# Recurrence of an RWKV-7 layer: the inverse's second direction moved to the array's off-diagonal quarters, work banks in two rotating pairs, side products for all 768 tokens at once

## What the reference computes

```python
def rwkv7_scan(S0, r, decay, k, v, kk, a, reverse):
    def step(S, inp):
        r_t, w_t, k_t, v_t, kk_t, a_t = inp
        sa = jnp.einsum('bhvk,bhk->bhv', S, -kk_t)
        S = (S * w_t[:, :, None, :] + sa[..., None] * (kk_t * a_t)[:, :, None, :]
             + v_t[..., None] * k_t[:, :, None, :])
        return S, jnp.einsum('bhvk,bhk->bhv', S, r_t)
...
    for d, rev in enumerate((False, True)):
        S_c, yc_d = rwkv7_scan(S0, r_c, d_c[d], k_c[d], v_c, kk_c, a_c[d], rev)
        _, yl_d = rwkv7_scan(S_c, r_l, d_l[d], k_l[d], v_l, kk_l, a_l[d], rev)
```

## Time and profile before

| | us |
|---|---|
| median of three executions | 2581.54 (2580.11 to 2587.41) |
| the profiled execution, its own time | 2585.16 |
| its span in the trace | 2583.6 |
| recurrence in the trace, its first products to its last | about 455 to 1121 |
| TensorE busy over the span | 2260.9 (88%) |

### The profile page before, as it was taken

How to read it: one execution, slowest core, us unless ns; L and a number is a source line. 1 busy time by engine, 2 the same in 40 slices (tenths; PEclk the granted TensorE clock), 3 DMA queues, 4 the chain that set the end, 5 groups by cost and what they waited for, 6 DMA issues and landing times. The chain is left out here.

```text
span 2583.6 us, 60917 instructions
## 1 busy us (share of the span) xinstructions
PE 2260.9 (88%) x26659; PEld 1830.6 (71%) x26659; DVE 1146.9 (44%) x1601; ACT 799.4 (31%) x1329; POOL 451.9 (17%) x335
## 2 busy tenths in 40 slices
PE   5899994788888998869799999999696778899998
PEld 3677782677777777757688888888563436688887
DVE  4633322666776667532422222222386652433333
ACT  2223322344334433221522112211433331542231
POOL 0222312644555446300000000000120000000000
PEclk8799896899999999989899999999798989999999
DMA  9566652000000000031122212121110002233332
GB/s 307 173 209 185 192 179 70 23 24 10 30 30 24 30 10 10 10 140 47 49 65 65 72 51 65 57 75 37 44 50 0 0 0 82 73 100 95 98 103 85
DMA packets 261822, 191.73 MB, mean 74 GB/s; under 512 B 11610, under 2 KB 252132, under 8 KB 261092
## 3 DMA queue, kind: packets, MB, share of 16 engines
q1 hardware_dynamic: 261604, 188.45, 24.0%
HBM read 170.60 MB, written 17.83 MB: 73 GB/s over the span
## 5 line engine op out<-in xcount | busy, mean ns | idle before, releaser
L486 DVE TENSOR_TENSOR ffn_lo<-ffn_raw,ffn_hi 128x1024 fp32r<-128x1024 f32 (+1 forms) x120 | 159.8, 1332 | 571.4 <-ACT ffn_hi L481 571.4
L493 PE MATMUL bank<-operand_hi,ffn_hi 128*128 128x512 f32 (+1 forms) x1056 | 378.9, 359 | 24.6 <-DVE operand_lo L455 24.4
L494 PE MATMUL bank<-operand_lo,ffn_hi 128*128 128x512 f32 (+1 forms) x1056 | 378.1, 358 | 0.0
L495 PE MATMUL bank<-operand_hi,ffn_lo 128*128 128x512 f32 (+1 forms) x1056 | 375.0, 355 | 0.0
L481 ACT CAST ffn_hi<-ffn_raw 128x1024 fp32r<-128x1024 f32 (+1 forms) x120 | 136.4, 1137 | 531.3 <-PE bank L495 531.1
L1569 POOL TENSOR_TENSOR lvl<-sc_b,level_mask 128x512 f32<-128x512 f32 x144 | 192.9, 1354 | 320.4 <-PE bank L1158 297.5
L493 PEld LDWEIGHTS bank<-operand_hi,ffn_hi 128*128 128x128 f32 x1056 | 200.4, 190 | 61.8 <-issue 22.4
L495 PEld LDWEIGHTS bank<-operand_hi,ffn_lo 128*128 128x128 f32 x1056 | 200.2, 190 | 29.9
L494 PEld LDWEIGHTS bank<-operand_lo,ffn_hi 128*128 128x128 f32 x1056 | 200.7, 190 | 27.2
L494 PE MATMUL bank<-ffn_g_lo,ffn_hi 128*128 128x512 f32 (+1 forms) x528 | 188.0, 356 | 0.0
L493 PE MATMUL bank<-ffn_g_hi,ffn_hi 128*128 128x512 f32 (+1 forms) x528 | 187.4, 355 | 0.0
(11 more groups left out here) (244 smaller groups left out, 4519.3 us busy)
## 6 DMA issues: line engine op xcount, KB each, us to landing
mod_raw<-in_mod_w SPq DMA_DIRECT2D x96, 512.0 KB, 6.1
ffn_raw<-in_ff_w SPq DMA_DIRECT2D x88, 512.0 KB, 3.9
ffn_raw<-in_ff_w SPq DMA_DIRECT2D x32, 704.0 KB, 4.5
proj_raw<-in_rw_wr SPq DMA_DIRECT2D x8, 512.0 KB, 4.5
proj_raw<-in_rw_wk SPq DMA_DIRECT2D x8, 512.0 KB, 4.6
proj_raw<-in_rw_wv SPq DMA_DIRECT2D x8, 512.0 KB, 4.9
rwkv_out_raw<-in_rw_wo SPq DMA_DIRECT2D x8, 512.0 KB, 4.3
qk_w_raw<-in_at_wq SPq DMA_DIRECT2D x8, 512.0 KB, 3.8
```

The source lines that it names most:

```text
L486: signal(eng, eng.tensor_tensor(self.lo[s][:, 0:k_tiles, :], self.raw[s][:, 0:k_tiles, :], self.hi[s][:, 0:k_tiles, :].bitcast(F32), ALU.s ...
L493: pe.matmul(out, w[0], x[0], start=first, stop=False)
L494: pe.matmul(out, w[0], x[1], start=False, stop=False)
L495: return pe.matmul(out, w[1], x[0], start=False, stop=last)
```

## The change

In `t` and `y` the first direction stays on the diagonal quarters and the second goes to the off-diagonal ones. The product `t` of direction 1 lands on the other head's partitions, so `y` needs the inverse of direction 1 with its halves exchanged: ScalarE makes that copy after every level but the last (`swap`, two copies of 64 partitions by 256 columns, 5 times per group), and `y` waits for it. The inverse is stored direction by direction. Scores, turned keys, values, `t`, `y` and all side products rotate through two pairs of banks (`WORK = c.pair`, 1024 columns each), so there is one rotation instead of two. A side product is made for 768 tokens at once, in one place of the table, and read by one instruction. The products with values leave `y`: those for the next step's right-hand side are issued in `rhs`, those for its output in `u`, those for its state in `sy`, each between matmuls of the diagonal quarters. The turned keys are copied by one instruction of 1024 columns instead of two of 512.

```diff
+        inv_s = [sb(f"inverse_swapped{s}", [P, GROUP, CH]) for s in range(2)]
...
-        Y_BANK, CHAIN, B_BANK, K_BANK, WORK = c.bank[0:2], c.bank[2:4], c.bank[4], c.bank[5], c.bank[6:8]
+        Y_BANK, CHAIN, WORK = c.bank[0:2], c.bank[2:4], c.pair
...
-        PLACES = ({0: (0,), 1: (1, 2), 2: (3,), 3: (36, 4), 4: (5,), 6: (37, 8), 7: (9,), 8: (10,), 9: (6, 11), 11: (7,)},
+        MAPS = {2: 0, 4: 1, 8: 2, 10: 3}
+        PLACES = ({0: (0,), 1: (1,), 2: (2,), 4: (36, 4), 6: (37, 8), 8: (10,), 9: (6,)},
                   {0: (12, 13), 2: (14,), 3: (15,), 4: (16,), 5: (17,), 6: (18, 22), 9: (19, 23)},
-                  {0: (24, 25), 3: (26, 27), 9: (33, 34)})
+                  {0: (24, 25), 3: (26, 27), 9: (33,)})
...
-                if k in (4, 5):
-                    side(t, "y_norm", k - 4)
-                if k in (7, 8):
-                    side(t, "gate", k - 7)
+                if k == 4:
+                    side(t, "y_norm")
+                if k == 7:
+                    side(t, "gate")
...
+                            elif kind == "score":
+                                pe.wait_ge(masked, 4 * rest[0] + 2 * rest[1] + 2)
+                            elif kind == "side":
+                                was_read(pe, self.use, *rest)
                             else:
-                                was_read(pe, self.use, *rest)
+                                pe.wait_ge(tok_copied, self.use.of("turn", kind, *rest) + 1)
                         return WORK[n % 2]
...
-                        for w in range(2 * GROUP):
-                            for h in range(2):
-                                mm = pe.matmul(bank[half(h), w * CH:w * CH + CH], lvl[G.parity][n % 2][half(h), w, :],
-                                               inv_t[G.parity][half(h), w, :], start=True, stop=True)
+                        for q in range(GROUP):
+                            for e in range(2):
+                                w, out = GROUP * e + q, slice(512 * e + q * CH, 512 * e + q * CH + CH)
+                                for h in range(2):
+                                    mm = pe.matmul(bank[half(h ^ e), out], lvl[G.parity][n % 2][half(h), w, :],
+                                                   inv_t[G.parity][half(h), w, :], start=True, stop=True)
                         mm.then_inc(t_ready, 1)
...
                         pe.wait_ge(t_copied, self.use.of("t", G.g, n) + 1)
-                        if step:
-                            self.early_waits(*step)
-                        for w in range(2 * GROUP):
+                        pe.wait_ge(x_swapped, self.use.of("x", G.g, n - 1) + 1)
+                        for q in range(GROUP):
                             for h in range(2):
-                                mm = pe.matmul(bank[half(h), w * CH:w * CH + CH], t_sb[G.parity][half(h), w, :],
-                                               inv[G.third][half(h), w, :], start=True, stop=True)
-                            if step and w < 6:
-                                self.early_part(*step, w)
+                                pe.matmul(bank[half(h), q * CH:q * CH + CH], t_sb[G.parity][half(h), q, :],
+                                          inv[G.third][half(h), q, :], start=True, stop=True)
+                            for h in range(2):
+                                mm = pe.matmul(bank[half(h), 512 + q * CH:512 + q * CH + CH],
+                                               t_sb[G.parity][half(1 - h), GROUP + q, :], inv_s[G.parity][half(1 - h), q, :],
+                                               start=True, stop=True)
                         mm.then_inc(x_ready, 1)
...
+                    def swap(self, G, n):
+
+                        for h in range(2):
+                            ins = a.copy(inv_s[G.parity][half(1 - h)], inv[G.third][half(h), GROUP:2 * GROUP, :])
+                        ins.then_inc(x_swapped, 1)
+
+                    def level0(self, G):
+                        act.wait_ge(level0_done, G.g + 1)
+                        self.swap(G, 0)
+
+                    def y(self, G, n):
+                        if n < LEVELS - 1:
+                            act.wait_ge(x_added, self.use.of("y", G.g, n) + 1)
+                            self.swap(G, n)
```

More of the change, by code:

```diff
@@ L873, in score @@
             def score(G, i):
-                use.take("bank", "score", G.g, i)
+                use.take("work", "score", G.g, i)
                 E.score(G, i)
             def turn_keys(G):
-                use.take("bank", "keys", G.g), use.take("turn", "keys", G.g)
-                use.take("copy", "b", G.g), use.take("copy", "k", G.g)
+                use.take("work", "keys", G.g), use.take("turn", "keys", G.g)
                 E.turn_keys(G)
@@ L883, in turn_values @@
                 if G.j < 2:
-                    use.take("bank", "values", G.g), use.take("turn", "values", G.g), use.take("copy", "v", G.g)
+                    use.take("work", "values", G.g), use.take("turn", "values", G.g)
                     E.turn_values(G)
```

372 lines of the change are left out of this document (188 added, 184 removed).

## The result

The changed kernel takes 2613.74 us (median of 4 runs, 2602.59 to 2623.28), the kernel before 2583.36 beside it (4 runs, 2580.11 to 2587.41): 1.0114 times the time, 95% interval 1.0081 to 1.0146. The prediction had 2554 and 2518 to 2586. The profiled execution took 2602.59 us and is the fastest of its four; its span is 2601.0.

The account below looks back on a forecast made before the run. TensorE was taken to bound only some slots, a loop over four engines the others. Terms 20 + 6 + 1 + 4 - 1 - 2 = 28 us off 2585.16 gave 2557, median 2554, range 2518 to 2586.

Parts of the forecast that it names:

- The product: In the inverse, each 32-row `t` or `y` takes 0.50 us instead of 0.94, saving 0.44 us.
- the floor of 25 ns a matmul: For `t` and `y`, a skill's minimum start-to-start gap: 32 rows at least 0.80 us, saving 0.14; the prediction rejected it.
- the ceiling: Most TensorE time the shorter products could save: 240 products, 106 us.
- The value products: Moved from `y` into `rhs`, `u` and `sy`, taken to cost 0; if not covered, 36 us in 96 steps.
- The exchange: ScalarE's two copies after a level: 0.63 us each pair, 76 us in all, hidden except in two places.
- One rotation: Side products wait more for banks; in the readout slot delays of 0.5, 1.6 and 1.5 us, partly paid back.
- the prediction's slower rival: Whole-width side products ahead of the state update lengthen readout slots about 3 us, side-work slots about 1: 2592, chance 0.15.
- The clock: Over the slots, less TensorE work lowers the granted clock; taken as 2 us lost.
- the prediction's bound: Over the slots, the granted clock falls from 0.98 to 0.89, with 39 us kept for it.
- The sum: All slots, prologue, last readout and clock together: 28 us gained.
- The slot without side work: That kind of slot gains 2.1 us of 21.23, coming to 19.1 us.

Follow-up runs that it names:

- first step's wait away, exchanges at `t`'s copy: Changed kernel without TensorE's first-step wait for the previous step's state, each exchange moved right ahead of the next level's `t` copy: 2585.9 us.
- diagonal, first step's wait away: Changed kernel with both inverse directions on diagonal quarters, no exchange, and no first-step wait for the previous step's state: 2599.6 us.
- mended, diagonal: The mended kernel with both directions on the diagonal quarters again and no exchange: 2594.8 us, ratio 1.0028.
- mended: Changed kernel without the first step's wait, exchanges at `t` copies, readout slots' first scores behind `u`, bonus work later: 2577.6 us, ratio 0.9969 against before.
- changed, fillers of 64 columns: Changed kernel with 8 unused 64x64 matmuls ahead of each of two waits per chunk step: 2666.4 us, ratio 1.0325.
- mended, fillers of two columns: The mended kernel with 16 unused two-column matmuls ahead of each of two waits per chunk step: 2728.8 us, ratio 1.0535.

## Why the prediction was wrong, point by point

**The product** was right: a `t` of 32 rows is over in 0.46 us (start of what follows; predicted 0.50):

```profile
820.34 0.68 PE L1156 MATMUL bank_pair<-inverse_t,lvl 64*64 64x64 f32 x32
820.80 0.43 PE L1255 MATMUL bank<-rhs,inverse 64*64 64x64 f32 x8
```

and the floor of 25 ns a matmul from the Trainium skill, "TensorE: Matmul & The Clock Gate", section "Back-to-back issue gap", doesn't hold for four quarters, as the prediction had argued from the earlier trace rows.

TensorE's busy time fell by 62 us and not by the 106 of the ceiling. Part of the difference is the clock: at half speed a record of a diagonal `t` starts 52 ns after the one before it, at full speed 28. By an estimate from that, 83 us more at half speed with TensorE three quarters busy add some 30 us of busy time.

**The value products** at 0: right for the products, shown by moving them on the kernel before. The wait that came with them in the first step is a term of its own, below.

**The exchange** is the step that failed. The prediction sized it a little low (0.82 us a pair where it had 0.63 and at most 0.8; 403 ns a copy) and looked at what stands behind it in two places, the last step and the slot from 802.62. It did not look at what is *queued behind it* in the others. In the readout slot that is the square, on which the variance, TensorE and the next `rhs` hang. Its words "the exchange runs beside the 0.71 us transpose and is hidden" consider only `y` and leave out ScalarE's queue. The prediction had the sum for the variance 1.0 us later, by the banks; it came 2.8 us later against the copy of `u`, and the slot took 29.4 us in place of 26.2. Moving that one exchange gave back 25 us on the kernel before, moving all gave 26 in the changed one, of a loss of 29.

```profile
L1490 ACT COPY inverse_swapped<-inverse 64x256 f32<-64x256 f32 x226 | 91.1, 403 | 137.4 <-DVE inverse L1370 134.3 <-DVE inverse L1358 1.3
```

Of that row the busy 91.1 us tells little, and neither does the sum of 137.4 us in which ScalarE sat idle ahead of it: on the kernel before it is 153.4 us with the exchanges in this order and 143.3 with one of them behind the square, and those 10 us went with 20 us of the stage. The price lies in the few waits with urgent work behind them. With the exchanges at the copies the same row of that kernel reads

```profile
L1499 ACT COPY inverse_swapped<-inverse 64x256 f32<-64x256 f32 x226 | 91.2, 404 | 4.1
```

**One rotation** was priced at little outside the readout slot. Diagonal quarters, no exchange, no first step's wait, against the kernel before with its value products moved: 1.0056 against 0.9996, some 15 us for the rotation and the whole-width pieces together. By slots, readout 28.1 in place of 26.7, side work 31.3 or more in place of 30.5, the third kind level. That is the mechanism of the prediction's slower rival in part (its 3 and 1 us), but the pieces put back made it worse, so what costs is most likely the banks that the scores and keys lost, and not the width. The two differ in more than that, the wide copy of the turned keys for one, which no run tried alone. One of the places, the scores ahead of `u`, is seen in the trace and was put right there: 0.18%, 5 us, by ratios within each other's intervals.

**The first step's wait** was in the diff and missing in the prediction: 5 to 11 us (0.21% with the quarters, 0.41% without, each between ratios whose intervals overlap).

**The clock** came out near the prediction's bound, not as its term: the slots fell to 0.92 (0.89 was the bound) and half-speed time rose from 21 to 104 us. What that costs in all was not isolated. In the slots of side work it can be read: four without half-speed time took 28.8 to 29.7 us, the two with 6.8 and 10.2 us of it 32.5 and 32.1, so some 7 us for both. It is not the main reason for the long readout slots, since two thirds of it stayed in them when they became short.

**The sum**, by the ratios along one path of single steps from before: value products moved -0.04%; rotation and whole width, diagonal, +0.60%; quarters with the exchanges at the copies (which holds the pauses and the clock) -0.63%; the exchanges put where the change has them +1.00%; the first step's wait +0.21%. That is 1.14%, 29 us slower. The prediction had -28 us for all of it. The quarters brought 16, and three other parts took 47. Each step carries an interval of about 0.2% or more, and another order of the steps could share the sum out differently: on the kernel before, the exchanges alone cost 1.66%.

**The slot without side work**, predicted at 19.1, took 24.52 at full clock. There the answer is not in any queue. Its waits:

```profile
PE bank_pair L1166 <- issue: 3.6, 5, 1.9
PE bank_pair L1156 <- issue: 2.5, 3, 1.6
PE bank L1199 <- issue: 1.5, 1, 1.5
PE bank_pair L1143 <- issue: 0.7, 1, 0.7
```

8.3 us in all. Some 2 of them, at `y`, are the usual wait for `t`'s copy, which shows as "issue" before too: 1.5 in the same slot. The others, 6.4 us in five places, are pauses at a matmul that waits for no semaphore, four of them inside a product, as in this one of 32 rows. They are more than the 5.4 us by which the slot missed its prediction, and are described below.

```profile
1051.38 0.33 PE L1156 MATMUL bank_pair<-inverse_t,lvl 64*64 64x64 f32 x8
1052.43 0.58 PE L1156 MATMUL bank_pair<-inverse_t,lvl 64*64 64x64 f32 x24 [0.73 <-issue]
```

## What to carry to other kernels

Before an instruction that waits is put on an engine with room, write down what that engine issues next and who waits for *that*, for every place in which it is issued; the average load says nothing of it. Put such an instruction where its input is already there, right ahead of the copy whose reader also needs it.
When several uses share one rotation of buffers, look for a pair of uses that now wait for the same event, and issue the one on the critical path first.
Where an engine idles at an instruction that waits for no semaphore, lay the idle time beside the packets that carry its instructions before looking for the cause in the data.
Test a change of several parts by putting each part alone on the old kernel: here two such runs cleared one part and convicted another whose price had been taken from its duration.

## What the hardware did that was not expected

**Columns don't matter in a small product on two quarters.** 32 matmul records of 64 rows and 2 columns take 1.10 us (above), as long as 32 of 64 columns on the diagonal. On four quarters 32 of 64 columns take 0.46 to the next start. So at full clock the time goes with the instructions and with how many quarters take turns. The same section of the Trainium skill's "TensorE: Matmul & The Clock Gate" gives one gap of about 25 ns for 1 to 64 columns; from the first start of a product to its last, the traces have 28 ns a record for 2 columns on two quarters (median of 48 bursts), 28 to 29 for 64, and 15 for 64 on four quarters.

**TensorE pauses inside products, more often when they go over four quarters.** All inputs of a `t` are waited for ahead of its first matmul. Yet in the kernel with exchanges at the copies one stops after its first rows and goes on over 2 us later:

```profile
568.29 0.31 PE L1156 MATMUL bank_pair<-inverse_t,lvl 64*64 64x64 f32 x4
570.94 0.68 PE L1156 MATMUL bank_pair<-inverse_t,lvl 64*64 64x64 f32 x28 [2.34 <-issue]
```

Before `t` the waits for "issue" sum to 8.7 us in 10 places in the changed kernel, 9.5 in 7 in this one, 0.5 in one with diagonal quarters and no first step's wait. Over all lines of the stage, pauses of 0.5 us or more at a matmul for which no semaphore was waited are these:

| kernel | pauses | us |
|---|---|---|
| before | 6 | 6.6 |
| changed | 20 | 20.2 |
| first step's wait away, exchanges at `t`'s copy | 19 | 24.9 |
| diagonal, first step's wait away | 2 | 2.0 |
| mended, diagonal | 4 | 2.9 |
| mended | 12 | 17.0 |
| changed, fillers of 64 columns | 52 | 56.5 |
| mended, fillers of two columns | 46 | 51.0 |

The cause is very likely the supply of instructions. Those of TensorE come in packets of 16 KB,

```profile
q8 instruction: 183, 3.00, 0.5%
```

whose starts in the traces are never closer than 3.2 us, in any of the kernels looked at, and 4.0 to 4.6 us apart in the median. The traces' record of these packets fits the pauses without an exception: in all 17 kernels, each of the 257 such pauses ends 1.2 to 1.6 us after a packet has arrived. Of all starts of matmuls only about a tenth lie that far behind one, and so do only a tenth of the ends of waits of 0.5 us or more for a semaphore. In the case above the packet ran from 568.60 to 569.63 and TensorE went on at 570.94. Both runs with fillers also bear out that more instructions bring more pauses, 20 to 52 and 12 to 46, with 64 columns as with 2. No run changed the supply alone, so this is a close fit in time and not a test. The Trainium skill, "Runtime: NRT & Kernel Launch", section "Instruction fetch mechanics", says that instructions are refilled in 16 KiB blocks and that this is mostly hidden; the packets' size agrees, and if the cause is this one, "hidden" does not hold here.

**VectorE took twice as long beside GpSimd**: the same 128x768 operation takes 2.01 us while GpSimd cuts `lvl`, and 0.95 where no operation of GpSimd runs. In the stage the four of this line that lie beside GpSimd from start to end take 2.01 each, and the others 0.94 to 0.95. Why was not tried.

```profile
823.74 3.21 POOL L1591 TENSOR_TENSOR lvl<-sc_b,level_mask 128x512 f32<-128x512 f32 x2
...
825.75 2.01 DVE L1423 TENSOR_TENSOR k<-k,sig 128x768 f32<-128x768 f32 x1
...
833.90 0.95 DVE L1423 TENSOR_TENSOR k<-k,sig 128x768 f32<-128x768 f32 x1
```
